# A two-block transformer program: 128 of 512 tokens read their experts' rows from a table in DRAM, the dense expert products run for 384

## Reference

```python
def peer(h, p):
    q = (hf @ p['peer_w_q']).reshape(T, PEER_HEADS, 2, PEER_D_HALF)
    s = jnp.einsum('thpd,hpnd->thpn', q, p['peer_keys'])
    top_s, top_i = lax.top_k(s, PEER_TOPK)                      # 16 of 128, for each of 8 heads and 2 halves
    cand_s = top_s[:, :, 0, :, None] + top_s[:, :, 1, None, :]
    cand_i = top_i[:, :, 0, :, None] * PEER_N_KEYS + top_i[:, :, 1, None, :]
    best_s, best_pos = lax.top_k(cand_s, PEER_TOPK)             # 16 experts a head, 128 a token
    idx = jnp.take_along_axis(cand_i, best_pos, axis=-1)
    g = jax.nn.softmax(best_s, axis=-1)
    ...
    act = jax.nn.gelu(jnp.einsum('td,thkd->thk', xb, u_tab[ib]), approximate=False)
    return jnp.einsum('thk,thkd->td', gb * act, v_tab[ib])
```

## Time and profile before

| | us |
|---|---|
| median of the runs | 4180.51 |
| the profiled execution | 4183.62 |
| its span | 4181.8 |
| PE busy | 3916.4 |
| DVE busy | 2153.7 |
| ACT busy | 1316.7 |
| POOL busy | 1607.1 |

### The profile page before, as it was taken

One profiled execution on the slowest core, in us unless ns is written; L12 is line 12 of the kernel. 1 busy time (PEld: TensorE's weight loads), 2 busy tenths in 40 slices (PEclk: granted clock), 3 DMA queues, 4 the chain that ended last, 5 costly groups with the idle time before them and its releaser, 6 DMA issues.

```text
span 4181.8 us, 51355 instructions
## 1 busy us (share of the span) xinstructions
PE 3916.4 (94%) x17790; PEld 3114.6 (74%) x17790; DVE 2153.7 (52%) x3709; ACT 1316.7 (31%) x1692; POOL 1607.1 (38%) x653
## 2 busy tenths in 40 slices
PE   8999988999998999688989999989899999999999
PEld 5777667777876877366767767778778888878887
DVE  4330444222245421666565526999884444357775
ACT  4332342333433222232334422235552222221211
POOL 5774342232343434133321234332224444444453
PEclk9999999999999999799999999999999999999999
DMA  5553222222432333122221323335555333435553
GB/s 160 159 156 110 76 92 68 76 93 72 144 123 76 96 100 102 41 66 78 94 80 60 108 80 123 118 104 177 177 176 166 113 113 108 143 120 188 200 174 131
DMA packets 201136, 485.23 MB, mean 116 GB/s; under 512 B 14185, under 2 KB 80681, under 8 KB 196299
## 3 DMA queue, kind: packets, MB, share of 16 engines
q1 hardware_dynamic: 175520, 429.77, 32.3%
q10 hardware_dynamic: 25450, 53.37, 3.6%
HBM read 418.07 MB, written 65.01 MB: 116 GB/s over the span
## 4 chain that ended last, share of the span: by engine, by line
PE 33%; DVE 12%; issue 3%; DMA 2%; DVEq 1%; ACT 0%; SPq 0%; POOL 0%; ACTq 0%; POOLq 0%
PE bank L501 9%; PE bank L503 9%; PE bank L502 9%; PE bank L1011 2%; DMA expert_gelu_ahead<-peer_gelu_ahead 2%; DVE expert_act L2241 1%; PE bank L747 1%; PE bank L712 1%; DVE one_hot_j L2214 1%; DVE matches L2201 1%; PE bank L602 1%; DVE expert_hi L2245 1%; DVE one_hot_i L2213 1%; DVE reciprocal_root L1647 1%; PE bank L985 0%
## 5 line engine op out<-in xcount | busy, mean ns | idle before, releaser
L460 POOL TENSOR_TENSOR weights_lo<-weights_raw,weights_hi 128x1024 fp32r<-128x1024 f32 x649 | 1606.8, 2484 | 2552.6 <-ACT weights_hi L1089 2551.9
L501 PE MATMUL bank<-operand_hi,weights_hi 128*128 128x512 f32 x2856 | 1154.4, 404 | 61.1 <-DVE operand_lo L1660 19.3
L1089 ACT ACTIVATE weights_hi<-weights_raw 128x1024 fp32r<-128x1024 f32 x649 | 682.2, 1057 | 1402.2 <-PE bank L503 1164.4
L503 PE MATMUL bank<-operand_hi,weights_lo 128*128 128x512 f32 x2856 | 1122.0, 393 | 0.0
L502 PE MATMUL bank<-operand_lo,weights_hi 128*128 128x512 f32 x2856 | 1122.0, 393 | 0.0
L501 PEld LDWEIGHTS bank<-operand_hi,weights_hi 128*128 128x128 f32 x2856 | 542.5, 190 | 189.9 <-DVE operand_lo L1660 25.5
L503 PEld LDWEIGHTS bank<-operand_hi,weights_lo 128*128 128x128 f32 x2856 | 541.2, 189 | 116.2
L502 PEld LDWEIGHTS bank<-operand_lo,weights_hi 128*128 128x128 f32 x2856 | 542.7, 190 | 110.1 <-issue 5.8
L501 PE MATMUL bank<-expert_hi,weights_hi 128*128 128x512 f32 x1024 | 404.8, 395 | 7.1 <-DVE peer_sum L2253 6.9
L503 PE MATMUL bank<-expert_hi,weights_lo 128*128 128x512 f32 x1024 | 403.5, 394 | 0.0
L502 PE MATMUL bank<-expert_lo,weights_hi 128*128 128x512 f32 x1024 | 403.4, 394 | 0.0
(11 more groups left out here) (375 smaller groups left out, 4663.4 us busy)
## 6 DMA issues: line engine op xcount, KB each, us to landing
weights_raw<-in_w_ffn_gu SPq DMA_DIRECT2D x132, 512.0 KB, 3.5
weights_raw<-in_w_peer SPq DMA_DIRECT2D x112, 512.0 KB, 3.6
weights_raw<-in_w_peer_ahead SPq DMA_DIRECT2D x72, 512.0 KB, 3.8
weights_raw<-in_w_peer_out SPq DMA_DIRECT2D x72, 512.0 KB, 3.6
peer_gates<-gate_stage SPq DMA_DIRECT2D x32, 1024.0 KB, 4.8
expert_gates<-peer_gates SPq DMA_DIRECT2D x16, 2048.0 KB, 9.2
weights_raw<-in_w_ffn_down SPq DMA_DIRECT2D x44, 512.0 KB, 3.6
weights_raw<-in_w_dil SPq DMA_DIRECT2D x44, 512.0 KB, 3.6
```

Source lines behind the costliest of these rows:

```text
L460: pool.tensor_tensor(LO[:, slot, :], RAW[:, slot, :], HI[:, slot, :].bitcast(F32), ALU.subtract).then_inc(sem("lo_ready"), 1)
L501: pe.matmul(out, wh, hi(k), start=(k == 0), stop=False)
L503: ins = pe.matmul(out, wl, hi(k), start=False, stop=(k == kc - 1))
L1089: act.activation(HI[:, slot, :], RAW[:, slot, :], ACT.Copy).then_inc(sem("hi_ready"), 1)
```

## The change

Tokens 0 to 127 leave the dense method. A table in DRAM, `expert_table` [16384, 2048], holds for each expert its `u` row and its `v` row (8 KB). It is written while the earlier parts run:
- `u` half: 128 units are loaded a second time by ACT, turned in 32 x 32 pieces by one DVE transpose of [128, 1024], and stored by ACT in four DMAs (pieces of 1 KB). 40 units go with the first feed-forward's gate and up products (from its second turn), 24 with its down product, 40 with the second feed-forward, 24 with the query products. In the two gate and up parts there are two load buffers and one turned buffer; in the others two or four of each.
- `v` half: SP issues one copy from DRAM to DRAM (512 KB, pieces of 512 bytes) after each weight unit of the mixing parts, 128 in all.

In the first tile's top-k DVE also computes the 128 indices of each token. For each of 128 slots (8 heads x 16) POOL issues an indirect DMA that gathers one 8 KB row per token (1 MB, four buffers); DVE takes the dot products with the tokens, which lie in banks 5 and 6, ACT applies gelu and the gate, and DVE adds the weighted `v` row in banks 4 and 7. Twelve slots stand in each shared group, six or five in each out group but the last. The sum is turned by PE and added to the residual in the last group.

The dense products take the columns 128 to 511 alone. BY_TILE becomes 12 and GATE_TURNS 6; the first tile's transposes are of its tokens, not of its gates, and its scores' successor doesn't wait for `best_ready`. Two more edits in the dense part: casts to the high part move from DVE to ACT, and in the shared groups gelu and gates are applied within PSUM, so that DVE's subtraction reads PSUM. ACT's and DVE's loops there, and ACT's in the feed-forwards, are written out. The keys are loaded after the last table store.

```diff
-BY_TILE = 10
+BY_TILE = 12
-GATE_TURNS = 8
+GATE_TURNS = 6
+ND = TOK - P
+SLOTS = 8 * TOPK
+DEEP = 4
...
+def steps_of_group(g):
+    if g < SHARED:
+        return range(1, 7), range(9, 15)
+    if g < SHARED + AHEAD - 1:
+        return (range(1, 7) if (g - SHARED) % 2 == 0 else range(1, 6)), ()
...
+                if name in ("hg", "dil", "mq", "memkv", "gate1", "merge1", "wout1", "hyz", "naqkv"):
+                    while done < count:
+                        unit(src[first + done], n0 + done, (n0 + done) % RING)
+                        copy_values()
+                        done += 1
...
+            def gather(s):
...
+                if s >= DEEP:
+                    pool.wait_ge(sem("slot_used"), s - DEEP + 1)
+                pool.indirect_dma_start(RB[:, s % DEEP, :], None, TAB,
+                                        bass.IndirectOffsetOnAxis(ap=IDX[:, s:s + 1], axis=0))\
+                    .then_inc(sem(f"gathered{s % DEEP}"), 16)
...
+            for s in range(DEEP, SLOTS):
+                after.setdefault(dense + place_of[s - DEEP + 1] + 4, []).append(s)
...
                 for k in range(BY_TILE):
-                    block_(DC, *x_ops(), gate=True)
-                pe.wait_ge(sem("best_ready"), t + 1)
-                turn([IJG[:, i, :] for i in range(3)])
+                    block_(DC, *dense_ops(), width=ND, gate=True)
+                if t == 0:
+                    pe.wait_ge(sem("first_tile_ready"), 1)
+                    for c in (0, 4):
+                        turn([XS[:, c + i, :] for i in range(4)])
+                else:
+                    pe.wait_ge(sem("best_ready"), t + 1)
+                    turn([IJG[:, i, :] for i in range(3)])
...
+            def save_rows(which, j):
...
+                act.wait_ge(sem(f"rows_turned_{which}"), saves[which])
+                for q in range(4):
+                    act.dma_start(rows[4 * j:4 * j + 4, q, :, 0, :].rearrange("b x q -> x b q"),
+                                  src[32 * q:32 * q + 32, :].rearrange("p (b q) -> p b q", b=4))\
+                        .then_inc(sem(f"table_stored_{which}" + ("" if which == "gu" else str(i))), 16)
...
-            blocks(16)
+            for k in range(4):
+                load_rows("q", TABLE_WQ[k])
+            for m in range(16):
+                blocks(1)
+                for k in range(3 * m // 2, 3 * (m + 1) // 2):
+                    save_rows("q", TABLE_WQ[k])
+                    if k + 4 < len(TABLE_WQ):
+                        load_rows("q", TABLE_WQ[k + 4])
+            for i in range(4):
+                act.wait_ge(sem(f"table_stored_q{i}"), 64 * len(TABLE_WQ) // 4)
             act.dma_start(KEYS[:], a["keys"]).then_inc(sem("keys_loaded"), 16)
...
+            def turn_rows_gu(k, t, odd):
...
+                dve.wait_ge(sem(f"rows_loaded_gu{odd}"), 8 * before + half)
+                wait(dve, sem("table_stored_gu"), 64 * before + 64 * t)
+                turned_rows(UT, UR[odd]).then_inc(sem("rows_turned_gu"), 1)
...
+            def dot():
...
+                for h in range(2):
+                    rows = RB[:, r, TOK * h:TOK * h + TOK]
+                    ins = dve.tensor_tensor_reduce(rows, rows, BANK[5 + h][:], 1.0, 0.0, ALU.mult, ALU.add,
+                                                   DOT[:, r, h:h + 1])
...
+            def add_values():
...
+                        ins = dve.scalar_tensor_tensor(sums_of[h][:], rows, AW[:, r:r + 1], sums_of[h][:],
+                                                       ALU.mult, ALU.add)
...
+            def step(steps, u):
+                if u in steps:
+                    dot()
+                    if slots["dotted"] > 1:
+                        add_values()
...
+            for o in range(AHEAD - 1):
+                steps = steps_of_group(SHARED + o)[0]
                 for c in range(8):
+                    ahead_pieces(o + 1, c)
+                    add(c, s1 + UNIT * (c + 1) + 8 * UNIT * o)
+                    step(steps, c)
```

More of the change, by code:

```diff
@@ L1226, in ffn @@
                     units(4)
+                    act.wait_ge(sem("pe_steps"), UNIT * 4 * FC)
+                    for k in range(2):
+                        load_rows("down", TABLE_DOWN[k])
                 else:
@@ L1580, in _ @@
             n["unit"] += 4 * GATE_TURNS
-            n0 = n["unit"]
-            def gelus(g, shift):
+            act.wait_ge(sem("turned"), n["turn"])
+            for h in range(2):
+                for i in range(2):
+                    q = 2 * h + i
+                    act.activation(BANK[5 + h][:, 256 * i:256 * i + 256].rearrange("p (c y) -> p c y", y=32),
+                                   XT[:, :, 32 * q:32 * q + 32], ACT.Copy).then_inc(sem("tokens_ready"), 1)
+            done = {"slot": 0}
@@ new lines, in _ @@
+                        act.activation(bank, bank, ACT.Gelu).then_inc(sem("gelu_ready"), 1)
+                        if u:
+                            expert_high(WH[:, u - 1, :], BANK[(n0_block[0] + u - 1) % 4][:, 0:ND], 8 * g + u - 1)
+                    elif g == SHARED - 1 and u < 12:
+                        ahead_highs(0, u - 8)
+                    step(steps, u)
+            for o in range(AHEAD):
+                steps = steps_of_group(SHARED + o)[0]
+                for u in range(8):
+                    units(1)
+                    if o + 1 < AHEAD and u < 4:
+                        ahead_highs(o + 1, u)
+                    step(steps, u)
+                if o == AHEAD - 2:
+                    slot_gelu()
@@ L1706, in two_pairs @@
                 def two_pairs(i):
+                    first = isinstance(i, int) and i == 0
                     for p in range(2):
@@ L1736, in ffn @@
                 if k == 0:
-                    copy_blocks(YT, DC, FC, scaled=True)
+                    for m in range(DC):
+                        for t in range(3 * m, 3 * m + 3):
+                            turn_rows("down", t)
+                        copy_blocks(YT, 1, FC, first=m, scaled=True)
                     rstd(DC, D, TOK)
```

399 lines of the change are left out of this document (299 added, 100 removed).

## The result

The changed kernel takes 4050.9 us (median; 4047.2 to 4052.2), the kernel before on the same chip 4181.0. The ratio is **0.9688**, 95% interval 0.9673 to 0.9702: 130 us less. Forecast were 269 us less, 3912 us, with a range of 3840 to 4020. The sign was right, the size was half as large, and the time lies 31 us above the range.

The account below looks back on a forecast made before the run. The prediction took TensorE, busy for 94% of the span, to bound the kernel, with DVE bounding top-k. One-hot -107, dense stage -194 and table building +32 summed to -269 us, giving 3912 us, range 3840 to 4020.

Parts of the forecast that it names:

- rival E: Dense stage: matmul doesn't fall to three quarters, weight loads of 0.19 us pace it: +39, 3951 us; chance 0.03.
- B: Dense stage: each gather costs POOL 2.8 us, so shared groups take 72 us: 3944 us in all; chance 0.14.
- D: Dense stage: a gather holds POOL for 5.26 us and POOL sets the stage: +294, 4206 us, slower; chance 0.04.
- turn 1.2, hidden chain 4.1, turn 1.2, issues 1.8, landing 2: 10.3 us: Second feed-forward: table work per pair of blocks, just under the pair's 10.9 us; the stage was taken at +10 us.
- rival C: Table traffic: 1 KB-piece stores land at twice the time; second feed-forward +55, queries +25, first +10: 4002 us; chance 0.14.
- 9.8 us + 4 x 1.2: First feed-forward: DVE's work per turn of the loop with table turns; +5, with the down products +7 us.
- 334 GB/s in 67 us; the trace reaches 403: Shared groups: 22.5 MB a group fits the DMA rate, so the group stays PE's at 67.4 us.
- the forecast's own sign of being wrong: Shared groups: the forecast is wrong if POOL or DMA is behind PE's waits there.
- two sums that gave 40: Out groups: DVE's summed work and the loop through DMA each came to 40 us a group.
- The circle: Out groups, loop through DMA: load of gates and activations about 15 us, first to last product 25, together 40 us.
- again about 15: Out groups: after the last product, loading 3.1 MB of gates and activations beside gathers takes about 15 us, as now.
- DVE becomes the bound: Out groups: DVE's operations sum to 40 us a group where PE needs 33.7, so DVE sets the time.

Follow-up runs that it names:

- experiment 1: The changed kernel with two turned buffers in both feed-forwards in place of one (last four table units of each still through one): 3984.9 us.

## Why the prediction was right and wrong

**Right.** One-hot turns -107.9 us (forecast -107) and top-k +1.1 (0): DVE's own time, read from rows of the same operations. The matmul: starts are 0.174 us apart, forecast 0.1755, so rival E is out. A gather holds POOL for 0.955 us in the shared groups and up to 1.10 in the out groups, forecast 1.0, so rivals B and D are out. A reduction takes 0.68 us and a weighted addition 0.75, forecast 0.69. The hand-over to the out groups and the end came within some 3 us each.

**Right by luck.** Query products: +11.6 for +12, but the keys' lateness is worth 5.0 (forecast 9) and the bytes 6.7 (forecast 3).

**Wrong, second feed-forward, +49 for +10.** The step is "turn 1.2, hidden chain 4.1, turn 1.2, issues 1.8, landing 2: 10.3 us". It counts one landing in a pair of turns, as if the other lay under the hidden chain. With one buffer each turn has its own: 2 x (1.25 + 1.8 + landing). And the landing was 4.0 us, not 2, nearest to the upper row with 3.6. With the right count the lower row gives 10.1 us a pair, still under PE's 10.9, and the upper one 13.3, where the forecast had 11.9 for it. Measured were 13.1 and 13.4, and 20 pairs of +2.4 are 48. Count and row both had to be right to see it. The size is that of rival C, whose reason (stores landing at twice the time) was the nearest to the truth: its time of 4002 fell short by the first feed-forward and the out groups.

**Wrong, first feed-forward, +53 for +7.** It was priced by busy sums, "9.8 us + 4 x 1.2" of DVE in 26, without a wait. Three losses were in it: the landing again, 21.9 us; the modulation rows copied after a turn, for which PE waits ten times, 12.6 us with its end; 16 us in the down products. A wait costs more than its length: of the 36.7 us of the gate and up products 23 are idle time of PE, nearly all of it in front of those rows, and 14 are longer matmuls, with the clock granted at 0.95 on average for 0.99 before, and at its lower level in short stretches after the waits, 37 us in all for 7 before. The forecast had no term for that. Two ideas for the last were tried, the turns before the last copy and ACT's queue. Each moved waits about and left the sum (155.7 to 155.7 us, 153.3 to 152.9). **It stays open** what sets it: the engine rows show DVE waiting 90 us for loads of table rows there, with the DMA engines at 0.86 and 275 GB/s, while the gate and up blocks carry about as much (272 GB/s in experiment 1) at nearly no loss once their waits are gone.

**Wrong, shared groups, 70.9 us for 67.4** (first six on average). The step is "334 GB/s in 67 us; the trace reaches 403": it sets an average against a peak of 5 us. The stage comes to 309 GB/s with gathers of 1 MB, and without their bytes the groups take 67.1. PE waits there for weights_lo (10.9 of 14.7 us), behind ACT's casts, which wait 76.9 us for the loads of these weights: the forecast's own sign of being wrong. The Trainium skill's page "HBM Reference" (Specifications (TRN2)) says that a core streaming alone gets about 425 GB/s, and some 358 if its pair streams too. The trace's short stretches, up to 420 GB/s, agree with the first; so the second, which I quoted, was the wrong one to set beside one core. Means over the stages with the DMA engines busy for 0.8 of the time or more stayed at 256 to 360.

**Wrong, out groups, 43.6 us for 40.** The forecast had two sums that gave 40, and took their agreement for evidence. The circle was the right one, and the step that failed in it is the load, "again about 15": it was 20 to 21 us, because gathers and the first weights come beside it (14.4 to 17.0 without gathers). The product part was 22.5 or 24.2 us for 25, and of the kind that the forecast said: DVE's own work of three columns, with what POOL holds. 23.4 and 20.3 make a group of 43.7. The other step, "**DVE becomes the bound**", failed too: DVE is idle for 9 us of a group, PE waits for weights_lo alone, not for expert_lo or peer_sum, and taking the slots' work away hardly moves the time. Its sum of 40 was 5.5 us too high for this kernel (34.5); the sixteen held operations were 17.9 us for 20.2. It agreed with the circle by chance. Without gathers, where DVE is the bound, they take 20.5 and a group 36.6.

## What to carry to other kernels

With one buffer, count the full cycle (fill, issues, landing) for every use, and price a landing by the row with the same issue pattern. A stage is not free because each engine's busy sum fits: write down the circle of waits, and ask which work of another engine stands between its members. Here putting eight products ahead of the additions and slots gave 5 us a group, while taking away the slots' work, some 14 of DVE's 34.5 us, gave nothing: POOL's holds and waits filled the time. So look at what holds an operation, not only at what stands before it; a held one counts as busy. Bytes beside a critical load cost there even where the mean rate looks low.

## What the runs showed of the hardware

- A copy of two elements a partition between SBUF places lasted 4.8 us on DVE while POOL ran two subtractions; with a PSUM operand that did not occur. Subtractions of 128x384 with two SBUF inputs lasted 1.21 us on average in the changed kernel's out groups, 0.69 with the products first, and 0.55 in the shared groups with one input in PSUM.
- A gather of 128 rows costs POOL 0.95 us for 8 KB rows and 0.96 for 256-byte rows (shared groups).
- Four stores of 128 KB, in pieces of 1 KB, need 1.8 us to issue and 4.0 to land at 215 GB/s of traffic.
- In gaps of 7 to 9 us without a matmul PE's granted clock fell to 0.50 and stayed there for 7 to 10 us, 3 to 5 of them with matmuls: in the out groups a loss of 2 to 3 us each on top of the gap (44.1 - 33.3 of matmuls - 8.4 of waiting).
